# The last modulation group of layer 1 moved from TensorE to VectorE, the other groups two units a visit, and the next layer's filter half a stage later

## The reference

```
def _layer(x, xc, c_act, cctx_act, p, rope, last):
    mod = (c_act @ p['w_mod'] + p['b_mod'])[:, None, :]
    sh1, sc1, g1, sh2, sc2, g2 = jnp.split(mod, N_MOD, axis=-1)
    n_ctx_mod = 2 if last else N_MOD
    mod_c = cctx_act @ p['w_mod'][:, :n_ctx_mod * D_MODEL] + p['b_mod'][:n_ctx_mod * D_MODEL]
    ...
    h = _modulate(_rmsnorm(x, p['norm1_g']), sh1, sc1)
    proj = h @ p['w_in']
    ...                      # three mixers: Mamba-2 scan, attention, Hyena long convolution
    x = x + g1 * (jnp.concatenate([y_ssd, y_att, y_hy], axis=-1) @ p['w_out'])
    x = x + g2 * _swiglu(_modulate(_rmsnorm(x, p['norm2_g']), sh2, sc2), p)
    ...                      # layer 1: the same for the context tokens xc
```

## Time and profile before

| | |
|---|---|
| median of 3 runs | 1277.47 us (1276.66 to 1277.97) |
| the profiled execution's own time | 1277.61 us |
| its span, first to last instruction | 1275.8 us |
| TensorE (PE) busy | 1216.1 us, 95% |
| VectorE (DVE) busy | 781.1 us, 61% |
| ScalarE (ACT) busy | 521.4 us, 41% |
| DMA | 171.89 MB, mean 135 GB/s |

### The profile page before, as it was taken

One profiled execution on the slowest core, in us unless ns is written; L12 is line 12 of the kernel. 1 busy time (PEld: TensorE's weight loads), 2 busy tenths in 40 slices (PEclk: granted clock), 3 DMA queues, 4 the chain that ended last, 5 costly groups with the idle time before them and its releaser, 6 DMA issues. The chain is left out here.

```text
span 1275.8 us, 17575 instructions
## 1 busy us (share of the span) xinstructions
PE 1216.1 (95%) x7212; PEld 987.8 (77%) x7212; DVE 781.1 (61%) x1273; ACT 521.4 (41%) x903; POOL 1.8 (0%) x8
## 2 busy tenths in 40 slices
PE   5999999999999899999999999999988998999998
PEld 3666777777676687788888888668778687999997
DVE  5653347867866654587655556555589876555554
ACT  4353445442444433222223322446565354443444
POOL 0000000000000000000000000000000000000000
PEclk9999999999999899999999999999999999999999
DMA  9833244441111243455555554323334223555653
GB/s 338 275 115 128 69 159 137 133 148 50 34 34 34 67 115 96 148 193 186 186 181 177 198 190 152 87 66 100 99 105 127 67 51 109 185 184 183 182 171 127
DMA packets 132456, 171.89 MB, mean 135 GB/s; under 512 B 9332, under 2 KB 112406, under 8 KB 132376
## 3 DMA queue, kind: packets, MB, share of 16 engines
q1 hardware_dynamic: 131892, 170.58, 41.6%
...
## 5 line engine op out<-in xcount | busy, mean ns | idle before, releaser
L1697 DVE TENSOR_TENSOR w_lo<-w_raw,w_hi 128x1024 fp32r<-128x1024 f32 (+1 forms) x220 | 264.2, 1204 | 234.1 <-ACT w_hi L1338 233.1
L1338 ACT ACTIVATE w_hi<-w_raw 128x1024 fp32r<-128x1024 f32 (+1 forms) x220 | 228.6, 1042 | 398.1 <-DMA w_raw<-in_w_gu_dram 184.9
L680 PE MATMUL ps<-h_hi,w_hi 128*128 128x512 f32 (+1 forms) x896 | 310.6, 347 | 2.8 <-DVE qk L1884 1.7
L682 PE MATMUL ps<-h_hi,w_lo 128*128 128x512 f32 (+1 forms) x896 | 303.8, 339 | 0.0
L681 PE MATMUL ps<-h_lo,w_hi 128*128 128x512 f32 (+1 forms) x896 | 303.7, 339 | 0.0
L680 PEld LDWEIGHTS ps<-h_hi,w_hi 128*128 128x128 f32 x896 | 170.6, 190 | 33.1 <-issue 15.4
L680 PE MATMUL ps<-f_hi,w_hi 128*128 128x512 f32 (+1 forms) x544 | 188.0, 346 | 5.7 <-DVE att_lo L2232 2.7
L682 PEld LDWEIGHTS ps<-h_hi,w_lo 128*128 128x128 f32 x896 | 170.5, 190 | 18.9
L681 PEld LDWEIGHTS ps<-h_lo,w_hi 128*128 128x128 f32 x896 | 170.8, 191 | 17.3
L682 PE MATMUL ps<-f_hi,w_lo 128*128 128x512 f32 (+1 forms) x544 | 182.9, 336 | 0.0
L681 PE MATMUL ps<-f_lo,w_hi 128*128 128x512 f32 (+1 forms) x416 | 139.9, 336 | 0.0
...
## 6 DMA issues: line engine op xcount, KB each, us to landing
...
```

The lines of the kernel that those rows point to most:

```text
L680: mm(o, w_hi[:, i % RING, w], hi[:, 0:n], start=first and k == 0, stop=False)
L682: last = mm(o, w_lo[:, i % RING, w], hi[:, 0:n], start=False, stop=final and k == nk - 1)
L1338: A(w_hi[:, i % RING, w], w_raw[:, i % RING, w], ACT.Copy).then_inc(w_hi_done, 1)
L1697: TT(w_lo[:, i % RING, w], w_raw[:, i % RING, w], w_hi[:, i % RING, w].bitcast(F32), ALU.subtract).then_inc(w_lo_done, 1)
```

## The change

MODS_IN goes from 4 to 3: group 5 of layer 1, the gate of the feed-forward part, is no longer made by TensorE in "in", but by VectorE in gu0, with two streams, at v = 8, 10, 12 and 14, ahead of the six groups of layer 2 (MOD_SUMS = 8, SUM_GROUPS = 7), which keep their places. VectorE reads the result at v = V_GATE = 21. The 24 units left stand two to a visit, in slots 1, 3 and the even slots 6 to 24; before there were 32 units in 28 visits up to slot 29. The filter of layer 2 goes 36 pieces back, to v = 42, 45 and 48 to 51 in gu1, and its loads behind piece 1 of gu1, since one of its tiles lies where the second stream of m_acc does. wdt has one tile for each layer now and t_half another address.

```
--- before.py
+++ after.py
@@ -83,7 +83,7 @@
 
 S_TAPS, S_SUMS, S_SPEC = 6, 8, 9
 
-V_SINE0, V_SINE1, V_TAPS = 6, 9, 12
+V_SINE0, V_SINE1, V_TAPS = 42, 45, 48
 
 SMALL_LOADS, LATE_LOADS = 14, 5
 CONV_CHUNKS = sum(kind in ("xbc", "hy") for kind, _, _ in W_IN)
@@ -91,11 +91,12 @@
 
 
 MOD_COLS = D
-MODS_FIRST, MODS_IN = 2, 4
-MOD_AT = [1, 1, 3, 3] + sorted([*range(4, 30), 14, 18])
+MODS_FIRST, MODS_IN = 2, 3
+MOD_AT = [1, 1, 3, 3] + [s for s in range(6, 26, 2) for _ in range(2)]
 SINE_LOADS, TAP_LOADS = 6, 3
 
-MOD_SUMS = 16
+MOD_SUMS, SUM_GROUPS = 8, 7
+V_GATE = 21
 
 PAIRS_BEFORE = (0, 4 * T // P)
 
@@ -136,13 +137,13 @@
 def mod_sum_at(v):
 
 
-    return (v - MOD_SUMS) // 2 if MOD_SUMS <= v < MOD_SUMS + 48 and v % 2 == 0 else None
+    return (v - MOD_SUMS) // 2 if MOD_SUMS <= v < MOD_SUMS + 8 * SUM_GROUPS and v % 2 == 0 else None
 
 
 def mod_rows_at(v):
 
     m, left = divmod(v - MOD_SUMS - 8, 8)
-    return m if left == 0 and 0 <= m < 6 else None
+    return m if left == 0 and 0 <= m < SUM_GROUPS else None
 
 
 def mod_turn_at(v):
@@ -154,7 +155,7 @@
 def mod_streams(m):
 
 
-    return 2 if m < 2 else 1
+    return 2 if m < 3 else 1
 
 
 def mod_adds(j):
@@ -270,7 +271,8 @@
         modv = at("modv", 199.5, [DEPTH, MODB, 2])
         amod = at("amod", 200.25, [DEPTH, 2, KD, 2])
         qkg = at("qkg", 200.5, [DEPTH, 2, HD])
-        wdt, wdt_hl = at("wdt", 154, [8, 16]), at("wdt_hl", 201.5, [8, 32], F32R)
+        wdts = [at(f"wdt{l}", kb, [8, 16]) for l, kb in enumerate((154, 176))]
+        wdt_hl = at("wdt_hl", 201.5, [8, 32], F32R)
         m_row = at("m_row", 202.5, [CW])
         bc16 = at("bc16", 203.5, [DEPTH, 3, 16])
         hyc, eps1 = at("hyc", 203.875, [4]), at("eps1", 203.9375, [1])
@@ -292,7 +294,7 @@
         t_filt, t_sum, t_diff = at("t_filt", 104, [2, D]), at("t_sum", 112, [2, 512]), at("t_diff", 116, [2, 512])
         t_mod = at("t_mod", 148, [2, CW])
         t_hyb = at("t_hyb", 152, [512])
-        t_half, t_hyb1 = at("t_half", 152, [D]), at("t_hyb1", 178, [512])
+        t_half, t_hyb1 = at("t_half", 180, [D]), at("t_hyb1", 178, [512])
         t_sum1, t_diff1 = at("t_sum1", 164, [2, 512]), at("t_diff1", 168, [2, 512])
         t_w3, t_decay = at("t_w3", 156, [D]), at("t_decay", 160, [2, 512])
         t_arg, t_k, t_h = ([at(f"{name}{l}", kb + off, shape) for l, kb in enumerate((144, 172))]
@@ -462,9 +464,11 @@
                 sp.wait_ge(m_used, KD * MODS_IN)
                 if j >= 2:
                     sp.wait_ge(S["mod_added"], mod_adds(j - 1))
-                k0, c0 = 2 * (j % 4), j // 4 * MOD_COLS
+                k0 = 2 * (j % 4)
+                lm, group = divmod(MODS_FIRST + MODS_IN + j // 4, 6)
+                c0 = group * MOD_COLS
                 sp.dma_start(m_big[j % 2][:].rearrange("p (k n) -> p k n", n=MOD_COLS),
-                             w_mod[1].rearrange("(k p) n -> p k n", p=P)[:, k0:k0 + 2, c0:c0 + MOD_COLS]).then_inc(m_full[j % 2], 16)
+                             w_mod[lm].rearrange("(k p) n -> p k n", p=P)[:, k0:k0 + 2, c0:c0 + MOD_COLS]).then_inc(m_full[j % 2], 16)
 
             def load_sines(l, full):
 
@@ -482,7 +486,7 @@
 
             def load_wdt(l):
 
-                sp.dma_start(wdt[:], w_in[l].rearrange("(k p) n -> p k n", p=P)[:, :, OFF_DT:OFF_DT + 16])\
+                sp.dma_start(wdts[l][:], w_in[l].rearrange("(k p) n -> p k n", p=P)[:, :, OFF_DT:OFF_DT + 16])\
                     .then_inc(wdt_full, 16)
 
             def load_in(l, s):
@@ -554,7 +558,8 @@
                         load_w(g + s, src[:, 4 * half:4 * half + 4, col:col + CW], 4)
                         if l == 0 and mod_sum_at(ffn_slot(part, s)) is not None:
                             load_big(mod_sum_at(ffn_slot(part, s)))
-                        if l == 0 and part == 0 and s == RING:
+                        if l == 0 and part == 1 and s == 1:
+                            sp.wait_ge(S["rows_made"], 3)
                             load_sines(1, hyw_full)
                             load_taps(1)
                             load_wdt(1)
@@ -578,9 +583,9 @@
                 pool.wait_ge(wdt_full, 16 * (l + 1))
                 if l > 0:
                     pool.wait_ge(S["dt_psum"], l)
-                nc.gpsimd.tensor_copy(wdt_hl[:, :, 0:16], wdt[:]).then_inc(wdt_hi_done, 1)
+                nc.gpsimd.tensor_copy(wdt_hl[:, :, 0:16], wdts[l][:]).then_inc(wdt_hi_done, 1)
                 pool.wait_ge(wdt_hi_done, l + 1)
-                nc.gpsimd.tensor_tensor(wdt_hl[:, :, 16:32], wdt[:], wdt_hl[:, :, 0:16].bitcast(F32), ALU.subtract).then_inc(wdt_split, 1)
+                nc.gpsimd.tensor_tensor(wdt_hl[:, :, 16:32], wdts[l][:], wdt_hl[:, :, 0:16].bitcast(F32), ALU.subtract).then_inc(wdt_split, 1)
 
 
         @block.tensor
@@ -2149,7 +2154,7 @@
                 split_w(g0 + 2)
                 if l == 0:
                     dve.wait_ge(S["row_turned"], MODS_IN)
-                    read_mod(0, 16, MODB)
+                    read_mod(0, 16, MODB - KD)
                     p.chain(V.memset(m_pick[:], 0.0))
                     p.link(V.memset(m_pick[:, 0, 0:1], 1.0))
                     p.link(V.memset(m_pick[:, 1, 1:2], 1.0))
@@ -2318,6 +2323,9 @@
                                 half_taps((v - V_TAPS) // 2)
                             if l == 0 and mod_sum_at(v) is not None:
                                 add_mods(mod_sum_at(v))
+                            if l == 0 and v == V_GATE:
+                                dve.wait_ge(S["row_turned"], MODS_IN + 1)
+                                read_mod(0, MODB - KD, MODB)
                     g0, q0 = PLAN[l, f"down{part}"]
                     for s in range(12):
                         if s == 0:
```

## The result

The changed kernel takes 1268.29 us (median of 4 runs, 1266.66 to 1269.49), the kernel before beside it 1277.07 us (4 runs, 1275.65 to 1277.97): ratio 0.9927, 95% interval 0.991 to 0.9943. Run twice more it gave 0.9926 (0.9911 to 0.994) and 0.9921 (0.9902 to 0.9939). The forecast was 1267.6 us.

The account below looks back on a forecast made before the run. TensorE was taken to bound both stages, with VectorE's time free unless splits come late. -10.9 + 0.2 - 0.5 + 1.2 + 0.5 - 0.4 = -9.9 us, from 1277.5 to 1267.6 us; range 1264.5 to 1272.5 us.

Parts of the forecast that it names:

- "In", -10.9 + 0.2: TensorE in "in": fewer units, visits, turns and waits save 10.9 us; a longer wait for ysum adds 0.2.
- The price of a visit, 0.34: TensorE in "in": going to small work and back costs 0.34 us; one unit costs 0.77, the second 0.43.
- The waits: Slots 14 and 19 of "in": TensorE's 1.64 us of waits go, as loads are issued one and a half pieces ahead.
- The feed-forward part, +0.8: Layer 1's feed-forward part, TensorE: -0.5 gate wait, +1.2 sum, +0.5 turn, -0.4 filter places.
- the filter: Feed-forward part: moving layer 2's filter removes 0.5 us of gate wait and saves 0.4 at three places.
- the sum and turn: Feed-forward part: one more group's sum costs TensorE 1.2 us and one more turn 0.5.
- VectorE's cover: gu0, v = 8 to 15: VectorE's added 19.4 us stay hidden, with no TensorE idle at all.
- rival 2: gu0: VectorE's new visits make splits late; 1287.0 us with the whole 19.4 us uncovered; chance 0.04.
- Rival 1: "In": the mixer's chains take back 4 of the 10.9 us, giving 1271.6 us; chance 0.15.
- Rival 4: Clock at 84 to 88 us: slow stretch goes, 1266.0 us, or one more comes, 1269.2; chance beyond forecast 0.07.

Follow-up runs that it names:

- two kernels with short leads at four of six places: Kernel before with its 28 units of slots 4 to 29 in 14 visits: ratio 0.9987; changed kernel with its ten pairs on neighbouring slots: 1271.43 us.
- the filter experiment: Kernel before with only the filter of layer 2 moved to the second half of the feed-forward part: 1277.93 us, ratio 0.9992.
- the second trace of before: Kernel before run again without an edit for a second trace: 1280.23 us, span 1278.4.

## Why the prediction was right

- **"In", -10.9 + 0.2.** The two traces differ by 10.57 us, as if the step had been exact. With the lost clock taken off it is 263.5 less 253.4 to 254.1, 9.4 to 10.1 us, and the distances around the small work of slots 4 to 29, added up, give 10.2. So the step was half a microsecond too large, and the clock hid it; that part is luck. What is missing, in the distances: the visits behind the taps' products had cost only 0.57 us each, so the ones taken away were worth 0.2 us less; the wait for ysum grew by 0.4 and not 0.2; a wait at the first spectrum product (L813, "issue") is 0.1 longer; slot 14 kept 0.15 us of idle time in the first trace, 0.24 and none in the repeats, where I had taken the whole 1.39 away, but the waits for m_raw that went had cost 0.3 us more than their idle time, which about makes up for it. Turns give back about 0.2. The price of a visit, 0.34, was right where it was read, behind a state product and between large products, and wrong behind the taps. The taps' products use 64 partitions and not 128, so the cost may be there already; no run separates that.
- **The waits.** The reason given, that a lead of one and a half pieces is enough and half a piece isn't, held for the changed kernel, and for two kernels with short leads at four of six places. Its "at least 9 us" didn't hold where it mattered: in slot 14, the tightest, the loads are 6.4 us ahead, hardly over the 5.9 to 6.2 us that a pair took to land elsewhere. The size of the term is partly luck as well: the kernel before waits 1.64 us for m_raw in one execution and 0.91 in the other. The row of slot 3, where the load belongs to the untouched part, shows 0.47 us in one of three traces of the changed kernel.
- **The feed-forward part, +0.8.** Measured 390.1 and 390.6 against 390.9 to 391.1: +0.3 to +1.0, +0.9 between the first two traces. Split by the filter experiment and the first trace of before, the filter is -0.8 of a predicted -0.9, and the sum and turn are left with 1.7 of a predicted 1.7; by the second trace of before the filter is -1.3, so its share is known to half a microsecond only.
- **VectorE's cover.** TensorE doesn't wait between v = 8 and 15, nor with 9.0 us more on VectorE; rival 2 begins between that and 17.9 us more, and even there the late split costs 1.18 us and the late sum 2.85.
- **Rival 1** took 0.4 of its 4 us. **Rival 4**, the clock, was sized as one stretch more or less in slots 4 to 6, and that place did lose it in two of three traces of the changed kernel. What it missed is that the same happens at four more places of layer 2, some 1 us each, so that two profiles of one kernel differ by 2.6 us in span (1275.8 and 1278.4). The forecast leaned on one execution of before, which had two low stretches in layer 2 where its second had four. The steps as the traces give them, about -10.2 in "in" and +0.8 in the feed-forward part, are -9.4 us; the three ratios of 0.9921 to 0.9927 are -9.3 to -10.1 us, the forecast -9.9.
